# Modulation weights in chunks of 512 rows by 512 columns, multiplied with 512 moving columns an instruction

## The reference, cut to what matters

```python
mod = jax.nn.silu(c) @ w_mod[layer] + b_mod[layer]          # w_mod: 1024 x 6144
sh1, sc1, g1, sh2, sc2, g2 = jnp.split(mod[:, None, :], 6, axis=-1)
mod_c = jax.nn.silu(c_ctx) @ w_mod[layer] + b_mod[layer]
csh1, csc1, cg1, csh2, csc2, cg2 = jnp.split(mod_c, 6)
h = modulate(x, norm1_g[layer], sh1, sc1)
hc = modulate(xc, norm1_g[layer], csh1, csc1)
...
dn_ctx = deltanet_prep(qkv_c, ba_c, conv_seq, ...)          # context half of the delta rule
```

## Time and profile before

| | us |
|---|---|
| median of three runs | 1524.32 |
| lowest and highest of the three | 1516.70, 1524.67 |
| span of the profiled execution | 1517.4 |
| first stage ("pre"), from the start to the first projection of the layers | 236.3 |
| PE busy, share of the span | 1403.4 (92%) |

### The profile page before, as it was taken

The page is one execution under the profiler, slowest core; times in us unless marked ns, Lnnn a source line. Parts: engine busy times, 40 slices in busy tenths (PEclk is TensorE's granted clock), DMA queues, the critical chain, the costliest instruction groups (busy, mean ns, idle before and its releaser), DMA issues.

```text
span 1517.4 us, 27437 instructions
## 1 busy us (share of the span) xinstructions
PE 1403.4 (92%) x10988; PEld 1337.1 (88%) x10988; DVE 900.8 (59%) x1433; ACT 712.4 (47%) x1045; POOL 131.2 (9%) x110
## 2 busy tenths in 40 slices
PE   2897999979999988979999998998999999999997
PEld 2786989869999988968999997998998999899997
DVE  2856677666645577675554558755745466544554
ACT  3753545445444445464544445644324445443442
POOL 0015011030000010230000003010601000000000
PEclk8977999979999999979999998999999999999999
DMA  8642443514555463523555553444200555455550
GB/s 295 223 139 84 143 154 104 167 56 139 171 198 188 153 190 115 172 77 112 167 178 200 179 167 114 137 127 124 84 2 1 184 177 168 139 194 171 191 167 28
DMA packets 175847, 219.18 MB, mean 144 GB/s; under 512 B 5000, under 2 KB 159462, under 8 KB 175590
## 3 DMA queue, kind: packets, MB, share of 16 engines
q1 hardware_dynamic: 173986, 212.80, 42.9%
q10 hardware_dynamic: 1732, 4.59, 0.8%
HBM read 216.32 MB, written 1.05 MB: 143 GB/s over the span
## 4 chain that ended last, share of the span: by engine, by line
PE 75%; DVE 10%; issue 5%; DVEq 4%; ACT 3%; DMA 2%; POOLq 1%; ACTq 0%; POOL 0%; SPq 0%
PE bank L638 20%; PE bank L640 20%; PE bank L639 20%; DVE w_lo L629 3%; PE bank L837 3%; PE bank L847 3%; PE bank L1326 1%; DMA w_raw<-in_w_mod 1%; PE bank L856 1%; PE bank L1507 1%; ACT w_hi L620 1%; PE bank L1389 1%; DVE arena L2167 1%; DVEq L2127 1%; DVEq L2262 1%
## 5 line engine op out<-in xcount | busy, mean ns | idle before, releaser
L629 DVE TENSOR_TENSOR w_lo<-w_raw,w_hi 128x1024 fp32r<-128x1024 f32 (+1 forms) x406 | 491.0, 1251 | 181.0 <-ACT w_hi L620 173.1
L638 PE MATMUL bank<-act_hi,w_hi 128*128 128x256 f32 x1808 | 521.6, 289 | 28.6 <-DVE act_lo L2090 11.1
L640 PE MATMUL bank<-act_hi,w_lo 128*128 128x256 f32 x1808 | 517.0, 286 | 0.0
L639 PE MATMUL bank<-act_lo,w_hi 128*128 128x256 f32 x1808 | 516.8, 286 | 0.0
L620 ACT ACTIVATE w_hi<-w_raw 128x1024 fp32r<-128x1024 f32 (+1 forms) x406 | 405.0, 1041 | 156.0 <-PE bank L640 111.6
L638 PEld LDWEIGHTS bank<-act_hi,w_hi 128*128 128x128 f32 x1808 | 352.9, 195 | 34.4 <-issue 10.3
L639 PEld LDWEIGHTS bank<-act_lo,w_hi 128*128 128x128 f32 x1808 | 352.8, 195 | 0.1
L640 PEld LDWEIGHTS bank<-act_hi,w_lo 128*128 128x128 f32 x1808 | 352.4, 195 | 0.0
L638 PE MATMUL bank<-side_hi,w_hi 128*128 128x256 f32 x896 | 259.1, 289 | 5.2 <-DVE w_lo L629 5.2
L639 PE MATMUL bank<-side_lo,w_hi 128*128 128x256 f32 x896 | 254.7, 284 | 0.0
L640 PE MATMUL bank<-side_hi,w_lo 128*128 128x256 f32 x896 | 254.6, 284 | 0.0
(11 more groups left out here) (311 smaller groups left out, 1584.2 us busy)
## 6 DMA issues: line engine op xcount, KB each, us to landing
w_raw<-in_w_in SPq DMA_DIRECT2D x40, 1024.0 KB, 5.7
w_raw<-in_w_up SPq DMA_DIRECT2D x32, 1024.0 KB, 5.5
w_raw<-in_w_down SPq DMA_DIRECT2D x32, 1024.0 KB, 5.4
w_raw<-in_w_mod SPq DMA_DIRECT2D x24, 1024.0 KB, 5.3
w_raw<-in_w_ffn_in SPq DMA_DIRECT2D x22, 1024.0 KB, 5.2
w_raw<-in_w_gate SPq DMA_DIRECT2D x20, 1024.0 KB, 5.1
w_raw<-in_w_ffn_out SPq DMA_DIRECT2D x11, 1024.0 KB, 4.9
w_raw<-in_w_out SPq DMA_DIRECT2D x8, 1024.0 KB, 5.0
```

The costliest lines, as they stand in the source:

```text
L629: nc.vector.tensor_tensor(wlo[:, slot, 0:n], raw[:, l % RAW, n * half:n * (half + 1)], whi[:, slot, 0:n].bitcast(F32), ALU.subtract).then_ ...
L638: nc.tensor.matmul(o, ahi, bhi, start=start, stop=False, skip_group_check=True)
L639: nc.tensor.matmul(o, ahi, blo, start=False, stop=False, skip_group_check=True)
L640: return nc.tensor.matmul(o, alo, bhi, start=False, stop=stop, skip_group_check=True)
```

## The change

A chunk of `w_mod` is now 512 rows x 512 columns. Chunk m covers row half m % 2 and the column block j = m // 2, so that a partition reads four runs of 2 KB. PE multiplies it with 4 row tiles by 2 parts = 8 matmuls of 512 moving columns into a whole bank, 6 or 7 by the parity of j, and two chunks accumulate in one bank. There is one copy of 4 x 512 for two chunks, at the even steps. `mod_rows` has one place of 512 columns in the room of the two of 256, so the copy of block j now also waits until the columns of block j - 1 have been made (`mod_cols`). `mod_columns(j)` has four small matmuls and stands two blocks behind, in front of every second chunk, and after each of the two series there are two blocks left to do (2 and 3, 10 and 11). The waits of DVE count blocks (4 and 12) where they counted chunks (8 and 24). Bytes, chunks, splits and the places in `FILL` are what they were.

```diff
--- before.py
+++ after.py
@@ -516,7 +516,7 @@
         scr = [A(512) for _ in range(3)]
         DELTA_END = A.at
 
-        mod_rows = z_n[:, 2:4, :]
+        mod_rows = z_n[:, 2:4, :].rearrange("p a b -> p (a b)")
         sc_b, sc_p = pre_x[:, 0:4, :], pre_x[:, 4:8, :]
         fn_u = [kt[:, K["mask"][0] + 512 * c:K["mask"][0] + 512 * (c + 1)].rearrange("p (k t) -> p k t", k=2)
                 for c in range(2)]
@@ -540,7 +540,8 @@
             return w[r:r + 256, c:c + n].rearrange("(k p) n -> p k n", p=P)
 
         w_in2 = a["w_in_2"][0]
-        mod_src = [k_all(a["w_mod_2"][0], 256 * m) for m in range(MOD_CHUNKS)]
+        mod_src = [a["w_mod_2"][0][512 * (m % 2):512 * (m % 2) + 512, 512 * (m // 2):512 * (m // 2) + 512].rearrange(
+            "(k p) n -> p k n", p=P) for m in range(MOD_CHUNKS)]
         ctx_src = [k_all(w_in2, c) for c in (K2, K2 + 256, V2, V2 + 256)]
 
         def layer_src(layer):
@@ -1300,12 +1301,12 @@
             tr = lambda o, x: nc.tensor.transpose(o, x, ident)
             mods = [0]
 
-            def mod_columns(m):
-
-                pe.wait_ge(S("mod_copied"), m + 1)
-                for i in range(2):
-                    c = 2 * (2 * m + i)
-                    mm = nc.tensor.matmul(ps[3][:, c:c + 2], mod_rows[0:4, m % 2, P * i:P * (i + 1)],
+            def mod_columns(j):
+
+                pe.wait_ge(S("mod_copied"), j + 1)
+                for i in range(4):
+                    c = 2 * (4 * j + i)
+                    mm = nc.tensor.matmul(ps[3][:, c:c + 2], mod_rows[0:4, P * i:P * (i + 1)],
                                           col("mod_sum", 0, 2)[0:4, :], start=True, stop=True)
                 mm.then_inc(S("mod_cols"), 1)
 
@@ -1313,17 +1314,18 @@
 
                 m = mods[0]
                 mods[0] += 1
-                if 2 <= m < MOD_FIRST or m >= MOD_FIRST + 2:
-                    mod_columns(m - 2)
+                j, rows = m // 2, m % 2
+                if rows == 0 and (2 <= j < MOD_FIRST // 2 or j >= MOD_FIRST // 2 + 2):
+                    mod_columns(j - 2)
                 l = m if m < MOD_FIRST else m + CTX_CHUNKS
-                o = ps[6 + m % 2][0:4, 0:256]
+                o = ps[6 + j % 2][0:4, :]
                 for half in range(2):
                     slot = (2 * l + half) % PIECES
                     pe.wait_ge(lo_ready, pre_w.pieces(l, half))
-                    for k in range(4):
-                        f = 4 * half + k
+                    for k in range(2):
+                        f = 4 * rows + 2 * half + k
                         for w in (whi, wlo):
-                            mm = nc.tensor.matmul(o, mod_in[:, f, :], w[:, slot, 256 * k:256 * (k + 1)],
+                            mm = nc.tensor.matmul(o, mod_in[:, f, :], w[:, slot, 512 * k:512 * (k + 1)],
                                                   start=f == 0 and w is whi, stop=f == KT - 1 and w is wlo)
                     mm.then_inc(pieces_done, 1)
 
@@ -1359,12 +1361,12 @@
             full(nc.tensor.matmul(ps[b][:, 0:T], ones, z_n[:, 0, :], start=True, stop=True), b)
             for _ in range(2, MOD_FIRST):
                 mod_chunk()
-            for m in range(MOD_FIRST - 2, MOD_FIRST):
-                mod_columns(m)
+            for j in range(MOD_FIRST // 2 - 2, MOD_FIRST // 2):
+                mod_columns(j)
             features_first("x", xtok)
             pe_delta(pe, "ctx", pre_w, MOD_FIRST, "pre", filler("ctx", mod_chunk))
-            for m in range(MOD_CHUNKS - 2, MOD_CHUNKS):
-                mod_columns(m)
+            for j in range(MOD_CHUNKS // 2 - 2, MOD_CHUNKS // 2):
+                mod_columns(j)
 
 
             with pe.Fori(0, DEPTH) as layer:
@@ -1625,18 +1627,20 @@
                 m = done_chunk[0]
                 done_chunk[0] += 1
                 split_hi(act, pre_w, (m if m < MOD_FIRST else m + CTX_CHUNKS) + 1)
-                if m not in (0, MOD_FIRST):
-                    mod_copy(m - 1)
+                if m % 2 == 0 and m not in (0, MOD_FIRST):
+                    mod_copy(m // 2 - 1)
                 if m == MOD_CHUNKS - 6:
                     for k in range(KT):
                         nc.scalar.activation(in_hi[k], h[:, k, :], ACT.Identity,
                                              scale=vec[:, k:k + 1]).then_inc(S("n1_hi"), 1)
 
-            def mod_copy(m):
+            def mod_copy(j):
+                m = 2 * j + 1
                 l = m if m < MOD_FIRST else m + CTX_CHUNKS
                 act.wait_ge(pieces_done, pre_w.pieces(l, 1))
-                nc.scalar.activation(mod_rows[0:4, m % 2, :], ps[6 + m % 2][0:4, 0:256],
-                                     ACT.Copy).then_inc(S("mod_copied"), 1)
+                if j:
+                    act.wait_ge(S("mod_cols"), j)
+                nc.scalar.activation(mod_rows[0:4, :], ps[6 + j % 2][0:4, :], ACT.Copy).then_inc(S("mod_copied"), 1)
 
             split_hi(act, pre_w, 0)
             b = full("pre", "vec")
@@ -1661,7 +1665,7 @@
             nc.scalar.activation(neg_a[:, :], dn_rows[:, 0:8], ACT.Exp).then_inc(S("exp_a"), 1)
             for _ in range(2, MOD_FIRST):
                 mod_step()
-            mod_copy(MOD_FIRST - 1)
+            mod_copy(MOD_FIRST // 2 - 1)
             for k in range(KT):
                 act.wait_ge(S("dn_mt"), k + 1)
                 nc.scalar.activation(xhi[:, k, :], mt[:, k, :], ACT.Identity,
@@ -1670,7 +1674,7 @@
                 b = full("pre", f"x{c}")
                 free(nc.scalar.activation(h[:, 2 * c:2 * c + 2, :], pair(b), ACT.Copy), b)
             act_delta(act, "ctx", pre_w, MOD_FIRST, "pre", filler("ctx", mod_step))
-            mod_copy(MOD_CHUNKS - 1)
+            mod_copy(MOD_CHUNKS // 2 - 1)
             act.wait_ge(S("rope_arg"), 2)
             nc.scalar.activation(rope_s[:, :], rope_s[:, :], ACT.Sin)
             nc.scalar.activation(rope_c[:, :], rope_c[:, :], ACT.Sin)
@@ -2052,7 +2056,7 @@
                 n = V[norm]
                 v.scalar_tensor_tensor(gains[:, i, :], modc[:, tile:tile + KT, j], 1.0, vec[:, n:n + KT], ALU.add, ALU.mult)
 
-            dve.wait_ge(S("mod_cols"), MOD_FIRST)
+            dve.wait_ge(S("mod_cols"), MOD_FIRST // 2)
             dve.wait_ge(S("vec_ready"), 1)
             modulation(0, 16)
             dve.drain()
@@ -2063,7 +2067,7 @@
             modulated(xc, lambda k: gains[:, 1, k:k + 1], lambda k: modc[:, k, 1:2], ("dn_mt", "dn_hi"), "dn_act")
             dve.wait_ge(S("tables"), 16)
             dve_delta(dve, "ctx", pre_w, MOD_FIRST, "pre", filler("ctx", mod_step))
-            dve.wait_ge(S("mod_cols"), MOD_CHUNKS)
+            dve.wait_ge(S("mod_cols"), MOD_CHUNKS // 2)
             free(modulation(16, 48), 3)
             dve.drain()
             gain_of(2, "norm2_g_2", 32, 0)
```

## The result

Eleven runs of each kernel on the same chip gave a median of 1529.28 us (1521.06 to 1534.02) after, against 1520.35 us (1516.34 to 1525.98) before. The ratio is 1.0056, with a 95% interval of 1.0035 to 1.0077. So the change costs 5 to 12 us, where +1.8 was forecast. The time of 1529.3 lies within the range of the prediction (1516 to 1532) and under its bound for "slower" (1531.9). Against the 1520.35 beside it, it is 0.56% and so just beyond the half per cent that was called "no change", though the interval reaches down to 0.35%.

The account below looks back on a forecast made before the run. The first stage's chain of waits was taken to bound the change: loads and DVE early, mostly PE later. Terms -0.34 - 0.64 + 0.4 - 0.1 + 0.7 + 1.8 = +1.8 us gave 1526 us; own range 1524 to 1528, wider range 1516 to 1532.

Parts of the forecast that it names:

- signs of being wrong: Trace readings named beforehand as refuting the forecast, among them granted clock 0.50 beyond 147 us and ACT's first split before 22.3.
- Loads: Loads before chunk 0 and behind chunk 7: longer runs save 0.17 us each, 0.34 us together, ends 0 and 1.
- Rival 2: Start of the kernel: queues take turns by the packet, so chunk 0 lands 0.9 us sooner; 1525 us, chance 0.10.
- Matmuls of a chunk: Chunks from z1 on: eight 512-column matmuls beat sixteen of 256 by 0.08 us a chunk, 0.64 us over eight chunks.
- Small matmuls: Rows of eight records before z chunks: 0.4 us lost from z1 to z4, -0.1 us at z6 and u0.
- the DVE link: Inversion level where the chain runs over DVE and PE waits at 208.58 us: eats PE's gain at x4, z5, x5.
- End of the first series: Behind chunk 7: block 3's copy waits for block 2's columns; 0.7 us lost, between 0.3 and 1.0.
- End of the stage: Blocks 10 and 11: columns, copy, columns in sequence, 2.76 us where 0.98 stood; 1.8 us lost, between 0.9 and 2.2.
- the added wait: ACT's copy waits for columns, blocked from 229.3 to about 236.4 us at the end; later work covered by 2 us.
- Rival 1: At z1 the clock rises later: 1531 us if missed once, 1539 if twice; chance 0.08 each.
- Rival 3: Whole kernel: the runs lie as the fastest of three did, 1516.7 us, giving 1518.5 us; chance 0.27.

Follow-up runs that it names:

- e3: Kernel before with fourteen more small records, results unused, behind the last eight of the first stage: 1520.93 us, ratio 1.0004 to the kernel before.
- e6: Changed kernel with each matmul of 512 moving columns given as two of 256: 1528.59 us, ratio 1.0044 to the kernel before.
- e7: Kernel before, its chunks unchanged, with its small matmuls grouped in the changed places and four places for copied rows: 1526.88 us, ratio 1.0034.
- e10: Kernel before with four added small records, results unused, in front of the chunk at z1: 1520.72 us, ratio 0.9996 to the kernel before.
- e4: Changed form for the first series alone, chunks 0 to 7, the rest as in the kernel before: 1520.85 us, ratio 1.0007.
- e2: Changed kernel with two `mod_rows` places and small matmuls spread as four records before every chunk, twelve left at the end: 1523.63 us, ratio 1.0008.
- e8: Changed kernel with one row of eight small records moved from z1 to T3: 1523.46 us, ratio 1.0006 to the kernel before.
- e11: Changed kernel with four added small records, results unused, in front of chunk 23 at u0: 1526.95 us, ratio 1.0048 to the kernel before.
- e0: Changed kernel run again without an edit: 1527.71 us against 1522.71 for the kernel before, ratio 1.0042.
- e1: Changed kernel with two places in `mod_rows`, so ACT's copy no longer waits for `mod_cols`: 1525.47 us, ratio 1.0033 to the kernel before.
- e5: Changed form for the second series alone, the 16 chunks beside the delta rule; chunks 0 to 7 as in the kernel before: 1528.10 us, ratio 1.0042.
- e9: Changed kernel with the second series' small rows before odd chunks, half a block sooner, eight records left at the end: 1519.23 us, ratio 0.9976.

## Why the prediction was right or wrong

**The time.** 1526 us was forecast and 1529.3 measured, within the range, and that nearness is luck. The change was put 7.1 us too low (+1.8 against +8.9 between the medians), and the start 4.0 us too high: three runs gave 1524.32 for the kernel before, eleven gave 1520.35. The prediction took the 6.9 us between the profiled span and that median for a fixed distance. In every run on record the time is 1.75 to 1.94 us above the run's own span, so the profiled execution was a run of about 1519.2 us, 1.1 under the median of eleven; the other 5 us were the scatter of three runs. Nor was half a per cent the least that can be told from nothing: eleven runs a side gave an interval of 0.2% each way. Two of the signs of being wrong that the prediction named stand in the first profile, a granted clock of 0.50 beyond 147 us (from 236.7 on) and ACT's first split before 22.3 us (21.86). The second was set too near: e3, with the loads of the kernel before, had chunk 0 at 21.44.

**Loads.** It agrees in size. Over five profiles with runs of 1 KB the link to chunk 0 is 17.73 to 18.32 us, in the mean 18.03; over nine with runs of 2 KB 17.45 to 18.14, in the mean 17.80. That is 0.23 us for the first load, where 0.17 was forecast, with ranges that overlap. Rival 2 (0.9 us, the queues taking turns by the packet) is not seen: a difference between the first two profiles, 0.53, is within the scatter.

**Matmuls of a chunk.** The gain of 0.64 us did not come for the reason given; about half of it came for another. The overhead goes nearly by the column, the end of the range that I named and did not take: where no small row stands ahead, eight of 512 columns take 1.85 us, 231 ns each, and sixteen of 256 take 1.87 in e6 and e7, 117 ns each. There is a difference of 0.08 us, but it belongs to the hand-over from a small row and is saved only where no row stands ahead now (x1, x2, x3 and u0, some 0.3 us together). The reading that failed was one row, 1.93 us, of a chunk behind a small row, taken for the bare chunk. The Trainium skill (TensorE: Matmul & The Clock Gate, Back-to-back issue gap) gives an overhead of the same form, a fixed one for each matmul; by it 512 columns would take 216 ns, the columns over 2.4 GHz plus 2.5 ns. The trace has 231, so it disagrees there too.

**Small matmuls, and all from z1 to the state.** Forecast -0.3 us (0.4 for the rows, -0.1 at z6 and u0, -0.64 for the chunks), measured 0.28 + 0.46 - 0.16 = +0.6 in the first pair of profiles. Up to z5 PE had gained 0.36 us (60.17 before, 59.81 after), and the DVE link took it back, as the prediction said that it does, so that z6 begins 0.28 later. Behind it z6's row costs 0.46, its forecast 0.45. The 0.53 us that the missing row at u0 was to save came to 0.16: PE waits there for POOL's operand, 1.62 us now and 1.15 before.

**End of the first series.** Forecast +0.7 less 0.34 for the loads, measured -0.57 us in the first pair. The working of the end was right to 0.1 (two rows of 0.99 and 1.06 with a copy of 0.59 between), but chunk 7 ended 1.3 us sooner than I had it. The profile of the kernel before was a late one there: its small records were done at 58.8, and by the same code at 56.7 in e3 and 57.6 in e10. e4 shows no price for this half of the change (its interval allows 4 us, its profile has none from z1 on).

**End of the stage.** Forecast +1.8, measured 1.78 from the state to the projection (8.73 against 6.95). Right. The term that is missing stands right behind: the projection begins at 1.2 GHz and takes 13.2 to 14.7 us to L1379 and not 12.0. That happened in all nine profiles with sixteen or more small records in front of it, and in none of the five with eight or twelve. I looked at the rows for what waits there (the added wait, the sum of L2096) and not for the clock.

**Rival 1, the clock rises later.** Its mechanism is the other part of the loss, but its chance was put too low and its place too narrow. Of the seven profiles with the changed rows, two missed the rise at z1 by the whole of L848 (+4.7 us, where the rival had 4.9), three had it 0.5 to 0.8 us late, and two on time. Three of the seven had one more stretch at 1.2 GHz later in the inversion or u part (67.4 and not 65.9 us), four one at the state matmuls (+1.4). Of the profiles with rows at T3 only e2 missed the rise, and e8 had it 0.6 us late and the fall at the state matmuls besides.

**The sum.** In the mean of the seven against before: 1.9 us from z1 to z2, 1.2 to u, -0.1 to the state, 2.4 to the projection and 1.7 to L1379, 7.1 together. Some 2.4 of it is steady work (the end 1.8, z6 and z1's row, less the rows gone from x1 and u0), 1.5 the fall in front of the projection that comes each time, and some 3 the late rises and falls that come in some executions. So the step that failed is the last one: I summed on one profile and took the changed kernel's clock to be the same. That term stood at nothing and came to some 4.5 us in the mean, and the only rival that had it got a chance of 0.16 in two fixed sizes. The steady part, put at 1.8, came to 2.4. Rival 3, the lower run of before, was none: over the 113 runs of the kernel before that stand beside the experiments, the times fill 1514.6 to 1529.7 us without a gap, so there are not two levels to choose from.

**What stays open.** Why the row at T3 matters. The seven comparisons of kernels without it give 1.0033 to 1.0056, the six with it (of four or eight records) 0.9976 to 1.0008, whatever stands at z1. That this is the line between them was seen after the runs, and nothing tried it alone: a kernel with no row at T3 and four records at z1 was not run. One thing that could carry it is PE's wait for POOL ahead of the second group of L828 (L829), which lies between T3 and z1. The first of these rows is of the kernel before, the second of the changed one, the third of e11:

```profile
125.53 0.66 PE L828 MATMUL bank<-consts_sb,arena 128*128 128x128 f32 x4 [1.93 <-POOLq L1203]
...
123.47 0.66 PE L829 MATMUL bank<-consts_sb,arena 128*128 128x128 f32 x4 [2.39 <-POOLq L1204]
...
126.51 0.66 PE L829 MATMUL bank<-consts_sb,arena 128*128 128x128 f32 x4 [0.93 <-POOLq L1204]
```

The wait is 2.4 us in the changed kernel, e0, e1 and e7, longer than before. But it is only 0.93 to 0.96 in e5, e6 and e11, which have no row at T3 either, and e6 and e11 are the two that missed the rise. So a longer idle stretch there doesn't explain it. The Trainium skill (TensorE: Matmul & The Clock Gate, What's actually happening) says that the chip looks at TensorE's activity in windows that run freely, so that the same kernel sees the clock change at other points from run to run. That agrees with two profiles of one kernel with the rise at the end of the chunk in one and within L848 in the other; which rows tip it, and why, no run here shows.

## What to carry to other kernels

Where a small job is put in a queue that is on the path, first look for the places at which its engine waits anyway: four records more at u0 cost 0.15 us in e11's profile, where four elsewhere cost 0.5. Then ask what the order does to the clock, and not only what the job costs. With the rows half a block sooner, two of them at places where PE waits (T3 and u0) and eight records fewer at the end, the changed kernel was 8 to 10 us faster (e9 at 1519.2 us, the changed kernel at 1527.7 and 1529.3), and in one comparison slightly faster than the one before. Which of these moves did it was not taken apart. Where executions of the same kernel differ by up to 15 us, compare stretches between fixed marks over several profiles; a pair of profiles alone would have put this change at +1.8 us.

## What the runs showed of the hardware

Rows of float32 matmuls with two moving columns were followed by a fall of the clock without any long idle time: in nine of nine profiles the granted clock fell to 0.50 just behind sixteen or more such records, though PE had been busy 0.82 of the four microseconds from 232 to 236 in the changed kernel (0.77 and 0.49 of the last two). In e3, with 14 dummy records behind the eight and no pause, it fell too. In the five profiles with eight or twelve such records there it did not. Besides the row's own time the price is in the 256-column matmuls behind it, 0.21 us each and not 0.12.

Columns set the time of rounded-float32 matmuls at full clock, nearly whatever their number in an instruction: 117 ns for 256 and 231 ns for 512.
